# Differential attention: the score matmuls of an item's two maps alternate, 512 keys of both, then 256 keys of both

## What is computed

```python
def diff_attn_block(qb, keys, vals, lam):
    s = jnp.einsum('bqhmd,bkhmd->bhmqk', qb, keys).astype(jnp.float32) * (DIFF_HEAD_DIM ** -0.5)
    p = jax.nn.softmax(s, axis=-1)
    a = p[:, :, 0] - lam * p[:, :, 1]
    return jnp.einsum('bhqk,bkhv->bqhv', a.astype(vals.dtype), vals)
```

## Time and profile before

| what | value |
|---|---|
| median of 3 runs | 1870.52 us |
| lowest and highest of them | 1866.34 and 1871.33 us |
| span of the profiled execution, first to last instruction | 1876.8 us |
| PE matmul busy | 1717.6 us, 92% of the span |
| DVE busy | 804.7 us, 43% |
| ACT busy | 518.8 us, 28% |

### The profile page before, as it was taken

How to read it: one execution, slowest core, us unless ns; L and a number is a source line. 1 busy time by engine, 2 the same in 40 slices (tenths; PEclk the granted TensorE clock), 3 DMA queues, 4 the chain that set the end, 5 groups by cost and what they waited for, 6 DMA issues and landing times.

```text
span 1876.8 us, 37887 instructions
## 1 busy us (share of the span) xinstructions
PE 1717.6 (92%) x16822; PEld 927.4 (49%) x16822; DVE 804.7 (43%) x1484; ACT 518.8 (28%) x983; POOL 109.4 (6%) x144
## 2 busy tenths in 40 slices
PE   5999999999999999999999999999999977778786
PEld 3444566544546555556667667544454333323332
DVE  3853144656627456355654554344462211222210
ACT  3710254311127422354453341122231110101010
POOL 0000010010000000100000000000001101010100
PEclk8999989999989999999998998899999999999998
DMA  9121376351110030042221210356569999999997
GB/s 396 76 88 47 145 287 247 145 224 69 45 45 1 23 151 0 17 170 82 77 81 50 63 56 24 114 219 221 219 239 398 416 425 415 422 413 425 417 423 279
DMA packets 48360, 359.25 MB, mean 191 GB/s; under 512 B 8325, under 2 KB 8557, under 8 KB 28736
## 3 DMA queue, kind: packets, MB, share of 16 engines
q1 hardware_dynamic: 35792, 311.51, 41.2%
q0 software_dynamic: 12400, 45.27, 7.3%
HBM read 337.47 MB, written 27.32 MB: 194 GB/s over the span
## 4 chain that ended last, share of the span: by engine, by line
PE 74%; DMA 16%; ACT 4%; issue 3%; DVE 2%; POOL 0%; SPq 0%; ACTq 0%; DVEq 0%; POOLq 0%
PE psum L207 71%; DMA arena<-in_w 16%; PE psum L210 3%; ACT arena L204 3%; ACT L204 1%; DVE arena L154 1%; DVE arena L180 0%; DVE arena L164 0%; DVE arena L172 0%; DVE arena L160 0%; POOL arena L141 0%; DMA arena<-in_tok 0%; DVE arena L168 0%; DVE arena L159 0%; POOL out L149 0%
## 5 line engine op out<-in xcount | busy, mean ns | idle before, releaser
L207 PE MATMUL psum<-arena 32*32 32x16 f32 (+12 forms) x16178 | 1638.1, 304 | 145.2 <-DMA arena<-in_w 73.4
L207 PEld LDWEIGHTS psum<-arena 32*32 32x32 f32 (+5 forms) x16178 | 856.0, 135 | 876.3 <-issue 764.7
L204 ACT ACTIVATE arena<-psum 128x512 f32<-128x512 f32 (+5 forms) x334 | 171.4, 513 | 871.2 <-PE psum L207 670.7
L154 DVE TENSOR_TENSOR arena<-arena,psum 128x512 f32<-128x512 f32 (+3 forms) x128 | 64.9, 507 | 402.6 <-PE psum L207 209.2
L154 DVE TENSOR_TENSOR arena<-arena 128x512 f32<-128x512 f32 (+10 forms) x315 | 191.6, 608 | 31.0 <-ACT arena L204 14.7
L204 ACT ACTIVATE arena<-arena 128x512 f32<-128x512 f32 (+10 forms) x254 | 138.8, 546 | 177.7 <-DVE arena L154 41.9
L204 ACT ACTIVATE arena<-psum,arena 128x128 f32<-128x128 f32 (+3 forms) x221 | 111.7, 505 | 275.1 <-PE psum L210 135.5
L154 DVE TENSOR_TENSOR arena<-psum,arena 128x128 f32<-128x128 f32 (+3 forms) x116 | 47.4, 409 | 154.5 <-PE psum L207 141.3
L164 DVE SCALAR_TENSOR_TENSOR arena<-arena 128x512 f32<-128x512 f32 (+7 forms) x162 | 103.5, 639 | 14.5 <-ACT arena L204 8.1
L210 PE MATMUL psum<-arena 128*128 128x128 f32 x644 | 102.6, 291 | 6.1 <-ACT arena L204 3.2
L172 DVE RECIPROCAL arena<-arena 128x1 f32<-128x1 f32 (+4 forms) x71 | 79.1, 1113 | 63.0 <-ACT arena L204 59.2
(11 more groups left out here) (49 smaller groups left out, 177.7 us busy)
## 6 DMA issues: line engine op xcount, KB each, us to landing
arena<-in_w SPq DMA_DIRECT2D x127, 2048.0 KB, 34.5
arena<-in_w SPq DMA_DIRECT2D x48, 256.0 KB, 3.1
arena<-in_w SPq DMA_DIRECT2D x12, 1024.0 KB, 36.4
arena<-kd POOLq DMA_DIRECT2D x28, 256.0 KB, 3.4
gd<-arena SPq DMA_DIRECT2D x24, 256.0 KB, 3.2
arena<-gd SPq DMA_DIRECT2D x24, 256.0 KB, 5.6
arena<-in_w POOLq DMA_DIRECT2D x2, 2048.0 KB, 9.6
kd<-arena POOLq DMA_DIRECT2D x2, 1536.0 KB, 11.0
```

Source lines behind the costliest of these rows:

```text
L154: return self.ends(self.e.tensor_tensor(out, a, b, op))
L204: return self.ends(self.e.activation(out, a, func, **kw))
L207: return self.ends(self.e.matmul(out, lhs, rhs, start=start, stop=stop))
```

## The change

In `diff_tensor` the waits for both maps' banks now come first. Then the four matmuls are issued with the keys outermost: 512 keys of the first map, 512 of the second, 256 of the first, 256 of the second. Each map's semaphore count is raised by its 256-key matmul, as before.

```diff
                     i, h = IT2[x]
                     for mp in range(2):
                         T.wait_ge(*ps.take(SPAIR, "s2", x, mp))
-                        b, r = ps["s2", x, mp], slice(64 * mp, 64 * mp + 64)
-                        T.mm(b[:, 0:512], QD[r, h, c4(i)], KD[r, h, 0:512], True, True)
-                        T.mm(b[:, 512:768], QD[r, h, c4(i)], KD[r, h, 512:768], True, True).then_inc("s2", x, mp)
+                    for keys in (slice(0, 512), slice(512, 768)):
+                        for mp in range(2):
+                            r = slice(64 * mp, 64 * mp + 64)
+                            T.mm(ps["s2", x, mp][:, keys], QD[r, h, c4(i)], KD[r, h, keys], True, True)
+                            if keys.stop == 768:
+                                T.then_inc("s2", x, mp)
```

## The result

The changed kernel took 1881.24 us in the median of 21 runs, the kernel before 1871.33 us in 21; the ratio is 1.0054, interval 1.0038 to 1.007. It is slower, by about 10 us where 5.25 were forecast, and a quarter of a microsecond beyond the range.

What follows compares the result with a forecast made beforehand. Neither PE nor ACT alone was taken to bound the stage, but a ring of items handing over between engines. Terms 2.85 + 1.32 + 0.42 + 0.66 gave +5.25 us on the 1870.52 us median: 1875.8 us, range 1869 to 1881.

Steps and rivals of the forecast that it cites:

- the mechanism: In the changed stage, the first map starts only at the second map's bank release; alternating the matmuls itself costs nothing.
- The ring of 4.72 us: One item's cycle at full clock: scores, reduce, first exponential, second exponential's read, bank release; 4.72 us against PE's 3.71.
- the rival's price: Rival that the old order ran the maps serially: alternation gains 16 x 1.07 = 17 us, 1853.4 us; chance 0.03.
- the sum for the stage: Added time over the changed stage's steps: 2.85 + 1.32 + 0.42 + 0.66 = +5.25 us.
- Steps from item 1 to 4: Three early steps between second-map bank releases: +2.85 us if all at low clock, +1.48 with one at full clock.
- Items 4 to 7: Three full-clock steps between bank releases: 12.84 us before, 14.16 in the new ring, +1.32 us.
- Squares and table loads: Steps from items 7 to 9 and 11 to 13, where ACT's other work covers the later scores: 0 us.
- Item 9 to 10: PE-bound step of 5.67 us before: +0.42 us at the low clock, -0.95 at full clock.
- Item 13 to 14: PE-bound step late in the stage: 4.06 us before, 4.72 after, +0.66 us.
- Items 10 and 14: Items whose two maps already started together in the kernel before, so their steps change by 0.
- so it goes through to the end: Behind the stage: the next stage's matmuls follow in program order on PE, so the whole +5.25 us reaches the end.
- My first rival: Low clock spreads in items 12 to 15, each further ring costing 1.37 us; 1878.5 us with two; chance 0.38.

Runs made afterwards that it cites:

- e4_after_p3: The changed kernel without any edit, profiled only, for a third profile at full clock; its stage took 87.18 us.
- the two changed kernels with delays: The changed kernel with two or four 128x512 matmuls added on PE behind the stage's loop; ratios to the kernel before 1.0051 and 1.0064.
- the delays above: The kernel before with five or ten 128x512 matmuls added on PE behind the stage's loop; ratios 1.0008 and 1.0049.
- the clock test: The kernel before with ten 128x512 matmuls into an unused bank, seven behind item 0's scores and three behind item 1's; ratio 1.002.

## Why the prediction was wrong in size, and where it was right

**Right: the mechanism.** The wait makes the loss and alternation nothing that shows (waits first 1.0044, alternation with the late wait 1.0004). The ring of 4.72 us stands at 4.71 with one wait and 4.77 with two; I had given the second wait instruction no price, and it takes some 0.06 us of every free step. The Trainium skill's rule of strict program order (TensorE: Matmul & The Clock Gate, Part 3) does not hold here: with the waits first, the old order needs 1.57 us for eight records, as alternation does with 1.56. (By that rule all four of the first map's records would have had to start ahead of the second map's first; I wrote three, which changes nothing in the rival's price.) With the late wait, too, the first map's 256 keys start at 568.06 us, ahead of the second 512-key record of the second map at 568.30, which stands before them in the program.

**Right: the sum for the stage**, though its terms were off both ways. Steps from item 1 to 4: 17.22 us, +1.80, where I took +2.85 with all three at the low clock and +1.48 with two. The third profile of the changed kernel (`e4_after_p3`) has all three at the low clock, 568.06 - 549.62 = 18.44 us, and its steps of 6.14 and 6.15 us are the ring that I had put at 6.09:

```profile
549.62 2.93 PE L207 MATMUL psum<-arena 64*128 64x512 f32 x8 [4.63 <-ACT arena L204]
555.76 2.93 PE L207 MATMUL psum<-arena 64*128 64x512 f32 x8 [3.21 <-ACT arena L204]
...
561.91 2.93 PE L207 MATMUL psum<-arena 64*128 64x512 f32 x8 [1.75 <-ACT arena L204]
...
568.06 1.56 PE L207 MATMUL psum<-arena 64*128 64x512 f32 x8 [1.07 <-ACT arena L204]
```

Which clock these items get differs between executions of one program, so this term has no single value. Items 4 to 7, in the first profile again: 14.48, +1.64 for 1.32; in it are the second wait instruction and a first step of 567.52 - 562.59 = 4.93 us, whose scores started late behind value products that had begun at the low clock. Squares and table loads: 0, as said; their cover held. Item 9 to 10: 594.52 - 588.83 = 5.69, PE bound, about 0 for +0.42. Item 13 to 14: 615.52 - 610.74 = 4.78 against 4.06, +0.72 for 0.66. Items 10 and 14: 0.1 together. Over all profiled executions with that stage unaltered, six with the kernel before's and five with the changed one's, its length is:

```
stage, us      kernel before and with a delay behind it   81.84 81.81 81.84 80.20 79.43 81.72   mean 81.1
               changed kernel and with a delay behind it  86.14 86.14 87.18 87.15 87.17         mean 86.8
```

The difference is 5.6 us; 5.25 was forecast.

**Wrong: "so it goes through to the end"**, that is, the step from the stage to the whole. The sum has a term for every step of the stage and puts what lies outside it at nothing, for the one reason that the next stage's matmuls stand behind this one's. Over the timed executions (157 of the kernel before, 31 of the changed) the means are 1869.9 and 1880.6 us, 10.7 apart with a standard error of 0.9; taken by rounds, 9.9 and 10.8. So some 5 us lie outside the stage (2 to 3, if the two changed kernels with delays are taken for it). They too come with the place of the wait: with the late wait the whole stands at 1.0004. The range had no part for them; it was made of the stage's bounds and the runs' scatter alone.

My first rival put a spreading low clock into items 12 to 15 of this stage. In the first profile these kept the full clock (0.63 us of idle before 615.52, then 1.56 for the scores). In the three profiles with stages of 87.2 us the steps from item 13 to 15 lost about a microsecond to it, but there the step from item 9 to 10 ran at full clock (4.8 us for 5.67), so the stage gained as much as it lost.

**Where these 5 us lie stays open.** Between the stage's tail and the end, the eleven profiles agree within 2 us everywhere but in the recurrent branch, which runs from 388 to 400 us in them (and took 404 with both waits first in the old order):

```
recurrent branch, us   before order   395.3 398.6 391.6 393.8 387.7 392.7   mean 393.3
                       changed order  396.7 396.2 399.9 392.3 390.2         mean 395.1
```

That scatter is as large as what is sought. With the added delays taken off, all that follows the stage means 1247.4 us before and 1249.5 after, with a standard error of 2.3 for the difference, so the profiles neither show the 5 us nor exclude them. And ahead of the stage, where the programs are the same, these executions take from 536.0 to 545.4 us: the span of one profile can be 9 us off before the change is reached.

Three explanations were tried, and none is shown. A later start: the delays above gave no regular loss beyond themselves. The clock: the mean granted clock of the timed executions is 0.9646 before and 0.9616 after, which with levels of 1.2 and 2.4 GHz is 2 x (1 - clock) of the time at the lower one, 132 and 145 us; across the executions of the kernel before a microsecond more at the lower level goes with 0.33 us more in all, which would make 4 us. But the profiles do not have it, neither in the stage (means of 16.0 and 17.8 us at the lower level) nor behind it (103.4 and 102.3), and the ten matmuls of the clock test gave the kernel before more time at full clock (0.9679) and no less time in all (1874.7). The wait instructions: taking out or putting in 15 of them moved some 2.6 us, of which 15 x 0.06 explains 0.9 in the stage at most, and neither shift is clear of the scatter. What the later stages do with a shift or a few instructions stays open at the level of 2 to 7 us.

No version beat the kernel before.

## What to carry to other kernels

Look at what the old order already overlaps before reordering matmuls: two records starting within 30 ns say that the pair is not waiting for a better order. Moving a wait up to join another moves everything between them behind the later of the two; if the work moved feeds the ring that produces that release, the ring gets longer, here from a mean of 4.28 to 4.77 us a step, and PE idles instead. For a change of a few tenths of a per cent, a stage's length from the trace is far steadier than the whole time, and a forecast of the whole needs a range for what lies outside the stage.

## What the runs showed that I had not expected

- A second wait instruction, on a value already reached, is not free where the engine has been waiting: two waits make a step of 4.77 us, one makes 4.71.
- A map's second matmul goes on while the other map's first, ahead of it in the program, still runs: with the late wait the alternating order lost nothing (steps of 4.30 us).
- Ten added matmuls held the clock of the kernel before at full speed through the whole stage and shortened it by 2.6 us, and the kernel was not faster (1.002).
- Ahead of the stage, where no instruction differs, the eleven profiles of the table above take from 536.0 to 545.4 us.
- The kernel before against itself gave 0.9978 with twelve runs: at this size the interval of one comparison is worth reading as such.
